# A sparse-attention decoder step on one core: the samples' index scores moved to the front, the prompt's index projections moved into the stage of the selection

## The reference, cut to what matters

```python
h = rmsnorm(x, W['mix_norm'][i])
aq, ak, av, iq, ik, iw, bq, bf, bi, bg = split(h @ w_in, IN_OFFSETS)
qi, ki = rope(iq, pos), rope(ik, pos)          # 8 heads x 64, and one shared key of 64
# scores: I[t,s] = sum_h w[t,h] * relu(qi[t,h] . ki[s])
# prompt: 1024 x 1024, causal.  sample: 4 queries x (8192 cached keys + 4 new ones)
_, idx = top_k(scores, 256)                    # then attention over the chosen keys alone
```

## Time and profile before

| | us |
|---|---|
| median of 3 runs | 3287.24 (3284.7 to 3288.15) |
| the profiled execution | 3285.84, its span 3284.0 |
| PE busy | 2955.7 (90%) |
| DVE busy | 1711.3 (52%) |
| ACT, POOL busy | 785.5 (24%), 492.2 (15%) |
| mean granted clock of PE | 0.952 |

### The profile page before, as it was taken

How to read it: one execution, slowest core, us unless ns; L and a number is a source line. 1 busy time by engine, 2 the same in 40 slices (tenths; PEclk the granted TensorE clock), 3 DMA queues, 4 the chain that set the end, 5 groups by cost and what they waited for, 6 DMA issues and landing times. The chain is left out here.

```text
span 3284.0 us, 41974 instructions
## 1 busy us (share of the span) xinstructions
PE 2955.7 (90%) x17344; PEld 2528.2 (77%) x17344; DVE 1711.3 (52%) x2105; ACT 785.5 (24%) x1121; POOL 492.2 (15%) x490
## 2 busy tenths in 40 slices
PE   6898999889688869999999999993699999999988
PEld 3593444464366749899999999892499999999988
DVE  2059998987476553433433343647633334344454
ACT  2132441142255511311111111320211111111232
POOL 1422335566442221000000000000000000000000
PEclk8899999899899979999999999996799999999999
DMA  2252120356511132111111111111011111111011
GB/s 90 59 155 79 53 80 8 112 166 184 184 34 37 35 105 68 56 52 40 47 45 52 39 52 34 33 33 52 31 40 51 52 40 52 40 52 40 28 51 68
DMA packets 160300, 207.62 MB, mean 63 GB/s; under 512 B 17127, under 2 KB 121231, under 8 KB 160094
## 3 DMA queue, kind: packets, MB, share of 16 engines
q1 hardware_dynamic: 145253, 154.38, 14.6%
q0 software_dynamic: 14848, 50.34, 5.2%
HBM read 182.13 MB, written 22.78 MB: 62 GB/s over the span
## 5 line engine op out<-in xcount | busy, mean ns | idle before, releaser
L1998 PE MATMUL ps<-h_split,w_split 128*128 128x352 f32 x7488 | 1215.5, 324 | 17.6 <-DVE w_split L2468 8.2
L1998 PEld LDWEIGHTS ps<-h_split,w_split 128*128 128x128 f32 x7488 | 1206.2, 189 | 24.5 <-issue 12.2
L1998 PE MATMUL ps<-hidden,w_split 128*128 128x352 f32 x3456 | 566.1, 323 | 0.0
L1998 PEld LDWEIGHTS ps<-hidden,w_split 128*128 128x128 f32 x3456 | 558.0, 188 | 0.0
L433 PE MATMUL ps<-w_chunk,hT 128*128 128x512 f32 (+3 forms) x1008 | 402.0, 553 | 26.7 <-DMA w_chunk<-in_w_in 26.7
L433 PEld LDWEIGHTS ps<-w_chunk,hT 128*128 128x128 f32 (+1 forms) x1008 | 169.9, 183 | 234.4 <-issue 202.8
L2506 DVE TENSOR_TENSOR xT<-xT,ps 128x1056 f32<-128x1056 f32 x176 | 220.5, 1253 | 203.0 <-PE ps L1998 202.8
L2485 DVE TENSOR_TENSOR hT<-hT,ps 128x1056 f32<-128x1056 f32 x44 | 55.0, 1254 | 361.2 <-PE ps L1998 361.2
L2359 ACT CAST w_split<-hT 128x2048 fp32r<-128x2048 f32 (+1 forms) x82 | 145.4, 1773 | 388.1 <-PE ps L1998 388.1
L2468 DVE TENSOR_TENSOR w_split<-hT,w_split 128x2048 fp32r<-128x2048 f32 (+1 forms) x82 | 175.0, 2134 | 80.4 <-ACT w_split L2359 79.2
L2495 DVE TENSOR_TENSOR hT<-hT,ps 128x1056 f32<-128x1056 f32 x44 | 55.2, 1255 | 233.4 <-PE ps L1998 233.4
(11 more groups left out here) (339 smaller groups left out, 3107.1 us busy)
## 6 DMA issues: line engine op xcount, KB each, us to landing
hT<-in_w_up SPq DMA_DIRECT2D x44, 1024.0 KB, 5.1
hT<-in_w_down SPq DMA_DIRECT2D x22, 1024.0 KB, 4.8
w_chunk<-in_w_in SPq DMA_DIRECT2D x6, 2048.0 KB, 8.4
hT<-in_w_ple_gate SPq DMA_DIRECT2D x16, 512.0 KB, 3.8
x_rows<-in_x_prompt SPq DMA_DIRECT2D x8, 512.0 KB, 4.5
w_gate_tile<-in_w_in SPq DMA_DIRECT2D x8, 512.0 KB, 5.3
w_out_raw<-in_w_out SPq DMA_DIRECT2D x8, 512.0 KB, 4.3
x_rows<-in_x_prompt SPq DMA_DIRECT2D x16, 256.0 KB, 2.6
```

The source lines that it names most:

```text
L1998: m = pe.matmul(out, w[a], x[b][:, g * GC:(g + 1) * GC], start=first and i == 0, stop=last and i == 2)
```

## The change

`load_normalised` and the stage of the projections of `iq` and `ik` are gone. `score_sample`, now in one stage with `lower_bound`, normalises the rows itself: the samples' tile first, the prompt's eight tiles between its other steps, the last six of them one in every two steps of the scoring loop. It loads the weights of `iq` and `ik`, projects the samples' 32 rows, rotates them on POOL, and scores. `select_sample` gets the prompt's jobs of `iq` and `ik` ahead of the others, eight each (61 jobs instead of 45), and the scores' steps begin at the third job of `av`. `EARLY_BIT` falls from 21 to 9.

```diff
-    jobs = [(c, r) for c in chunks for r in range(NT + 1)]
+    jobs = [(c, r) for c in chunks for r in range(NT if c in ("iq", "ik") else NT + 1)]
...
+        plain = starts[[c not in rotated for c in chunks].index(True)]
+        first = plain + LAG - 1
     def score_steps(j):
-        return range(2 * j, 2 * j + 2) if scores and 2 * j < len(index.steps) else range(0)
+        at = 2 * (j - first) if scores else 0
+        return range(at, at + 2) if scores and 0 <= at < len(index.steps) else range(0)
...
             for u in score_steps(j):
+                if u == 0:
+                    pe.wait_ge(copied, unplain)
                 index.tensor(pe, u)
...
-EARLY_BIT = 21
+EARLY_BIT = 9
...
 def score_sample(k, ctx, block):
     @block.sync
+        sp.dma_start(rows[0:NS, 0, :], io["x_sample"]...).then_inc(x_landed[0], 16)
+        sp.dma_start(w_iq, w_in[:, :, COL["iq"]:COL["iq"] + 512]).then_inc(w_landed[0], 16)
+        sp.dma_start(k.part[:], io["c_part"]).then_inc(pt_landed, 16)
         for s in range(8):
             sp.dma_start(pages[s:P:8, :]..., src).then_inc(pt_landed, 16)
+        sp.dma_start(w_ik[:], ...)
+        ...                                    # tables, x tiles 1 and 2
+        sp.wait_ge(iw_taken, 1)
+        ...                                    # the weights' round trip, the new index keys out
+        for t in range(3, NT + 1):
+            load_x(t)
     @block.gpsimd
+        for j in range(4):
+            gather(j)
+        rotate(0)
+        rotate(1)
+        for j in range(4, N):
+            gather(j)
     @block.tensor
+        turn_x(0)
+        project(0, w_iq, 512)
+        project(1, w_ik, IK_COLS)
+        turn(0)
+        turn_x(1)
+        turn(1)
+        turn_x(2)
+        ...                                    # turn the samples' key and queries, the new scores
+        for j in range(2, N + 2):
+            if j > 2 and j % 2 and LEAD + j // 2 - 1 <= NT:
+                turn_x(LEAD + j // 2 - 1)
             ...                                # turn(j), multiply(j - 2)
     @block.vector
         dve.wait_ge(pt_landed, 144)
         dve.tensor_scalar(index[:], pages[:], 8.0, k.part[:, 0:1], ...)
+        scale_x(0)
+        copy_x(0)
...
-    project_rows(k, ctx, block, chunks, scores=True, moves={3 * (NT + 1) + 1: move_lists})
+    project_rows(k, ctx, block, chunks, scores=True, moves={2 * NT + 3 * (NT + 1) + 1: move_lists})
...
-                    k.stage((load_normalised,), (lower_bound,))
-                    k.stage((project_rows, ["iq", "ik"]))
-                    k.stage((score_sample,))
-                    k.stage((select_sample, ["av", "bi", "bg", "aq", "ak"]))
+                    k.stage((lower_bound,), (score_sample,))
+                    k.stage((select_sample, ["iq", "ik", "av", "bi", "bg", "aq", "ak"]))
```

More of the change, by code:

```diff
@@ L172, in load_constants @@
     k.lb_logit = [k.vec[:, 8 * KD + i * BH:8 * KD + (i + 1) * BH] for i in range(2)]
[L177 to L243, removed]
@@ L334, in project_rows @@
     w_in = io["w_in"][0].rearrange("(k p) n -> p k n", p=P)
-    jobs = [(c, r) for c in chunks for r in range(NT + 1)]
+    jobs = [(c, r) for c in chunks for r in range(NT if c in ("iq", "ik") else NT + 1)]
+    starts = [jobs.index((c, 0)) for c in chunks] + [len(jobs)]
     rotated = {"aq", "ak", "iq", "ik"}
@@ L343, in project_rows @@
         index = k.index = PromptScores(k, ctx)
-        assert all(c not in rotated for c, _ in jobs[0:len(index.steps) // 2])
+        plain = starts[[c not in rotated for c in chunks].index(True)]
+        first = plain + LAG - 1
+        assert all(c not in rotated for c, _ in jobs[plain:first + len(index.steps) // 2])
     def score_steps(j):
-        return range(2 * j, 2 * j + 2) if scores and 2 * j < len(index.steps) else range(0)
+        at = 2 * (j - first) if scores else 0
+        return range(at, at + 2) if scores and 0 <= at < len(index.steps) else range(0)
     nth_rot, nth_store = {}, {}
@@ L371, in project_rows @@
     stored = k.sem_ring(ctx, "rows_stored", RAW)
-    projected, taken, roped, turned, copied, iw_stored = k.sems(
-        ctx, "projected", "taken", "roped", "turned", "copied", "iw_stored")
+    projected, taken, roped, turned, copied = k.sems(ctx, "projected", "taken", "roped", "turned", "copied")
+    chunk_of = [i for i in range(len(chunks)) for _ in range(starts[i], starts[i + 1])]
+    unplain = sum(starts[0] <= j < plain for j in nth_rot) if scores else 0
     def stores_before(j):
@@ L416, in turn @@
             pe.wait_ge(roped, t + 1)
-            if scores and t == 0:
+            if scores and t == unplain:
                 pe.wait_ge(index.rectified, len(index.steps))
@@ L483, in _ @@
     def _(pool):
-        if scores:
-            for u in range(len(index.steps)):
-                index.pool(pool, u)
         for j, (c, r) in enumerate(jobs):
+            if scores and j == plain:
+                for u in range(len(index.steps)):
+                    index.pool(pool, u)
             if c not in rotated:
@@ L1313, in score_sample @@
 def score_sample(k, ctx, block):
-    io, ps = k.io, k.ps
+    io, ps, hT = k.io, k.ps, k.hT
     N = BD * 4
     E16 = PAGE // 8
+    order = [NT] + list(range(NT))
+    LEAD = 3
+    w_iq = k.qT[:].rearrange("p f n -> p (f n)")[:, 0:KD * 512].rearrange("p (d n) -> p d n", d=KD)
+    room = k.kT[:].rearrange("p f n -> p (f n)")
+    rows = room[:, 0:3 * D].rearrange("p (s n) -> p s n", s=3)
+    square = room[:, 3 * D:4 * D]
+    stat = k.sb(ctx, "x_stat", [P, 3, 3])
+    w_ik = k.sb(ctx, "w_ik", [P, KD, IK_COLS])
+    raw = k.sb(ctx, "index_raw", [NS, 512 + DH])
+    rot = k.sb(ctx, "index_rot", [NS, 512 + 2 * DH])
+    rope_part = k.sb(ctx, "rope_part", [NS, 2, 512])
     pages = k.sb(ctx, "pages", [P, N], I32)
@@ L1359, in _, with gather @@
         view = io["cache_kidx"][0].rearrange("g (s e) d -> (g s) (e d)", s=8)
-        pool.wait_ge(indexed, 1)
-        for j in range(N):
+        def gather(j):
             if j >= 4:
@@ L1366, in _, with rotate @@
                                     ).then_inc(g_landed[j % 4], 16)
+        def rotate(n):
+            heads = 1 if n else H
+            cols, at = heads * DH, 512 * n
+            pool.wait_ge(taken, n + 1)
+            x = raw[:, at:at + cols].rearrange("p (h t d) -> p h t d", h=heads, t=2)
+            table = k.rope[0:NS, NT, :].rearrange("p (a t d) -> p a t d", a=2, t=2)
+            for a, v in ((0, x), (1, x[:, :, ::-1, :])):
+                pool.tensor_tensor(rope_part[:, a, 0:cols].rearrange("p (h t d) -> p h t d", h=heads, t=2), v,
+                                   table[:, a, :, :][:, None, :, :].broadcast_to([NS, heads, 2, DH // 2]), ALU.mult)
+            pool.drain()
+            if n:
+                pool.tensor_tensor(rot[:, at + cols:at + 2 * cols], rope_part[:, 0, 0:cols], rope_part[:, 1, 0:cols], ALU.add)
+            pool.tensor_tensor(rot[:, at:at + cols], rope_part[:, 0, 0:cols], rope_part[:, 1, 0:cols], ALU.add).then_inc(roped, 1)
+            pool.drain()
@@ L1368, in _ @@
+        pool.wait_ge(indexed, 1)
+        for j in range(4):
+            gather(j)
+        pool.wait_ge(sample_table, 16)
+        rotate(0)
+        rotate(1)
+        for j in range(4, N):
+            gather(j)
     @block.tensor
     def _(pe):
[L1370 to L1374, removed]
@@ L1375, in _, with turn_x @@
-        pe.matmul(ps[0:NS, 6, 0:NS * H].rearrange("p (b q) -> p b q", b=BD), k.ikT[0:DH, SEQ:R],
-                  bd[0:DH, :, 0].rearrange("p b t h -> p b (t h)"), start=True, stop=True).then_inc(new_scored, 1)
+        def turn_x(t):
+            r = order[t]
+            n = rows_of(r)
+            pe.wait_ge(x_scaled, t + 1)
+            if t:
+                pe.wait_ge(x_copied, t)
+            if t == LEAD:
+                pe.wait_ge(new_summed, 1)
+            for d in range(KD):
+                m = pe.transpose(ps[:, 6 + d // 4, (d % 4) * P:(d % 4) * P + n], rows[0:n, t % 3, d * P:(d + 1) * P], k.ident[0:n, 0:n])
+            m.then_inc(x_turned, 1)
@@ L1378, in turn, with project @@
+        def project(n, w, cols):
+            pe.wait_ge(w_landed[n], 16)
+            for d in range(KD):
+                m = pe.matmul(ps[0:NS, 2 + n, 0:cols], hT[:, d, SEQ:R], w[:, d, :], start=d == 0, stop=d == KD - 1)
+            m.then_inc(projected, 1)
         def turn(j):
@@ L1414, in _, with root, copy_keys @@
     def _(act):
-        for j in range(N):
+        def root(t):
+            n, s = rows_of(order[t]), t % 3
+            act.wait_ge(x_landed[s], 16 * (t // 3 + 1))
+            if t >= 3:
+                act.wait_ge(x_scaled, t - 2)
+            act.activation(square[0:n], rows[0:n, s, :], ACT.Square, accum_out=stat[0:n, s, 0:1])
+            act.drain()
+            act.activation(stat[0:n, s, 1:2], stat[0:n, s, 0:1], ACT.Sqrt, bias=k.eps[0:n, 0:1], scale=1.0 / D).then_inc(rooted, 1)
+        def copy_keys(j):
             for a in range(2):
```

123 lines of the change are left out of this document (98 added, 25 removed).

## The result

The changed kernel takes 3337.72 us (median of 4 runs, 3336.55 to 3340.04) where the kernel before took 3285.97 (4 runs beside it, 3283.25 to 3288.15): a ratio of 1.0159 [1.0141, 1.0176], slower. The forecast was 3327, its range 3308 to 3348. The profiled execution of after took 3336.55 us, with a span of 3334.8: 50.8 more than before.

A forecast was written before the change was run, and what follows sets the result against it. PE was taken to bound the scoring loop, PE and DVE together the selection, DVE ending it by some 4 us. Front -103.9, wait +73.2 and rounds +70.4 sum to +39.7 us: forecast 3327, range 3308 to 3348.

The forecast's parts named there:

- The front: Up to the selection's start: first weighing 110.1 us earlier, six tiles' transposes +6.2, so selection 103.9 us earlier, bounds 92 to 112.
- a sign that the prediction named for being wrong: Scoring loop: the forecast is wrong if its steps are longer than before by more than the transposes.
- rival 3: Front gains 22 us less, from a late page table and uncovered DVE and ACT tile work: 3349 us; chance 0.08.
- rival 4: Front gains more and the rounds are as short as they can be, 8 us: 3318, inside the forecast's range.
- The place of the lists: SP's queue in the selection: the lists stay behind the stores of `av`, `bi`, `bg`, which come 76.0 us later.
- the last turns of `ik`: PE in the selection: these turns and a wait for their copies add an estimated 1.1 us.
- The wait: DVE in the selection, ahead of the merge: a new wait of 73.2 us for the lists, bounds 68 to 78.
- The twelve rounds: End of the selection: twelve added threshold rounds without cover, 5.87 us each, 70.4 us; upper bound 81.6.
- The attention: Attention stage: loses twelve rounds, DVE idles about 96 us instead of 25.6, no gain counted, about 242 us as before.
- rival 2: Attention stage gives something back, at the very most PE's idle 32.7 us there: 3294; chance 0.04.
- Rival 1: Selection: the lists come in time, without the wait of 73 us; sum -15, 3272 us; chance 0.06.
- The spread: The forecast's own spread, 3312 to 3342 us, from the bounds of front, wait and rounds; chance 0.82.

The follow-up runs named there:

- the first experiment: Changed kernel with the DMAs of `cand` put ahead of job 34 and the spans' ahead of job 39, EARLY_BIT still 9: 3283.86 us, 0.9988 of the kernel before.
- the last experiment: Changed kernel with lists early, EARLY_BIT 21, seven table loads behind the first weights, and `ik` loaded ahead of `iq`: 3263.56 us, 0.9928 of the kernel before.
- The run before it: Changed kernel with lists early, EARLY_BIT 21, seven table loads behind the first weights, `iq` still ahead of `ik`: 3262.07 us, 0.992 of the kernel before.

## Why the prediction was right, step by step

**The front** was forecast to bring 103.9 us and brought 100.1. Its path was right to about a microsecond down to the first weighing (row numbers at 18.86 for 18.0, weighing at 47.08 for 46.0). The loop was not: from the first weighing to the last it takes 135.28 - 47.08 = 88.20 us, where it took 236.34 - 156.15 = 80.19 before, so 8.0 more instead of 6.2. 3.2 of them are the second step, 5.78 us behind the first (2.62 before), for which DVE waits 2.85 on PE. One of the six tiles lies in it, and PE works through it without a gap, but mostly at the lower of the clock's two levels; it had stood still three times for 1.3 to 1.8 us between 33.8 and 40.8. A tile's transposes in this step and in a later one, and the window of the step:

```profile
46.84 1.91 PE L1381 MATMUL ps<-ident,kT 128*128 128x128 f32 x8
...
55.49 1.09 PE L1381 MATMUL ps<-ident,kT 128*128 128x128 f32 x8
```

```profile
47.00:53.00 6.00, 6.00 (x37) 6.00 (x36) 2.74 (x4) 2.50 (x6) 0.93 (x1) 0.61 0.50 150
```

The kernel before was granted 1.00 in the same step (156 to 159 us). The other five tiles make a step 3.75 us instead of 2.62, 5.6 together, and one step at the end is 0.8 shorter. So the sum's 1.04 a tile was the price at the upper clock, and a sign that the prediction named for being wrong, a loop longer than before by more than the transposes, did come, by 1.8 us. DVE's and ACT's extra work was covered, as forecast (they are busy 72.19 and 50.62 of the 137 us from 6 to 143), so rival 3 falls; so does rival 4, the front being no better than the sum.

**The place of the lists**: 76.0 us of PE's added jobs were forecast, and `cand` was issued 80.6 later. The sum left out a queue: eight jobs of `ik` are short, so PE waits for their rotated keys,

```profile
228.71 1.90 PE L365 MATMUL ps<-w_chunk,hT 128*128 128x72 f32 x16
233.56 0.47 PE L354 MATMUL ps<-ident,rot 128*128 128x128 f32 x1 [2.95 <-POOL rot L442]
233.82 3.53 PE L365 MATMUL ps<-w_chunk,hT 128*128 128x72 f32 x16
```

and the tile behind that stop takes 3.53 us instead of 1.90, at a granted clock of 0.50 (233.6 to 237.4) instead of 1.00 (222 to 230). POOL itself was held up by ACT, which stood 6.2 us for a store of rotated keys:

```profile
231.79 0.18 ACT L392 ACTIVATE iw<-ps 128x8 f32<-128x8 f32 x1 [6.24 <-DMA out_kidx_prompt<-rot]
```

That store, issued at 223.90, stood behind the 2 MB of `av` in SP's queue (issued at 222.75). The small price for "the last turns of `ik`", 1.1 us, should have been some 6.

**The wait** was forecast at 73.2 us against where the lists stood before and measured at 77.5, in which DVE asked 5.5 us later, so that 72.0 are seen as idle time. (5.0 of the 5.5 lie in 16 pairs of short passes, L1645 and L1647, which take 8.4 and 11.7 us instead of 7.4 and 7.7; the prediction had DVE's passes unchanged.) The mechanism is the one named: with the lists issued early the wait is gone.

**The twelve rounds** were forecast at 70.4 us without cover, and the rounds cost 75.1 more. The size of the uncovered ones was right to the hundredth (597.06 to 602.93 is 5.87), and there were 13 of them; the ones beside POOL were sized too low, 6.8 where 9 rounds take (597.06 - 530.93) / 9 = 7.35. The average of before hid two kinds of rounds, and this is what is told of below. That the 5.87 was right is luck in part: the prediction read it in the earlier trace rows from the round that begins at 554.71, as one without rotations, but POOL rotated in that round too. POOL's timeline before, and DVE's at the end of the round:

```profile
555.29 2.50 POOL L502 TENSOR_TENSOR rope_part<-raw,rope 128x512 f32<-128x512 f32 x2 [3.56 <-ACT raw L459]
557.93 1.27 POOL L508 TENSOR_TENSOR rot<-rope_part 128x512 f32<-128x512 f32 x1
```

```profile
560.32 0.17 DVE L657 SCALAR_TENSOR_TENSOR threshold<-threshold,threshold_flip 128x6 int32<-128x6 int32 x1
```

The rotation ended at 559.20, before the round came to its two small updates (L655 at 560.08, then L657), and the round was as short as one without POOL.

**The attention** gave nothing back, so rival 2 falls: DVE's idle time ahead of the turned scores was 96.2 us with the rounds moved out and 23.7 with them in, as forecast, and the stage is 244 us either way. The gathers of keys after, in the list of a line's forms:

```profile
L1840 POOL DMA_INDIRECT gathered<-in_cache_k,slot_row x64: 940/953/2492, 676.4 to 790.0; - x64
```

Against 942, 952 and 2491 in the earlier trace rows: with none of the rounds beside them they are no quicker. The hold of GpSimd's gathers that the prediction took from the Trainium skill (SBUF — State Buffer, "SBUF: two separate sides") isn't seen here. The section itself gives the counting passes no such hold: it names VectorE's two-port modes for it, and leaves out of them the form of tensor_scalar that also writes out its accumulator, which these passes are.

**Rival 1**, the lists in time, wasn't this kernel but is the first experiment. It was priced at 3272, 15 below before, and came out 4.3 below. In that run the front is worth 4.2 less than in its sum (the selection starts at 143.93); the scores end 4.9 later against the selection's start (464.15 - 143.93 = 320.2 for 315.3, DVE waiting 7.0 for them); and the 22 rounds take 150.8 for 147. These three make 12.9 us where the time came out 10.7 above the rival's price.

The sum was +39.7 and the span says +50.8: 3.8 from the front, 4.3 from the lists and 4.7 from the rounds are 12.8 more; the way from the merge to the first round (57.4 us instead of 58.6) and the stage of the attention (244.5 instead of 245.0) take 1.7 back. The three errors point the same way, and the range, not the sum, took them in. The spread's upper end of 3342 was too low for its own bounds: 11.9 for the front, 4.8 for the wait and 11.6 for the rounds above 3327 make 3355.

## What to carry to other kernels

When work is added ahead of an entry in a queue that one engine goes through in order, ask who waits at the end of that entry: here 128 KB of lists (four DMAs of 32 KB) stood behind all the stores of `ik`, `av`, `bi` and `bg`, with which they had nothing to do. Moving them by ten jobs was worth 53.9 us with 22 rounds behind them, and 3.0 with ten. Work that is moved from a place where its engine idles to one where that engine ends the stage pays its full price there; here the place that it left gave nothing back. When two engines end a stage together, a repair of one chain is worth only what is left until the other ends it; size two repairs together before adding their gains.

## What the hardware showed that was not expected

**Rounds beside GpSimd take GpSimd's rhythm.** DVE's groups of the counting line and its two small updates, by form, from 531 to 597 (9 rounds beside rotations) and then from 597 to 673.6 (13 without), after (count | busy us, mean ns):

```profile
L571 DVE TENSOR_SCALAR_CACHE_REDUCE xT<-xT,threshold 128x1024 uint8<-128x1024 f32 x9 | 11.5, 1274 | 0.0
L591 DVE SCALAR_TENSOR_TENSOR threshold<-threshold,threshold_flip 128x6 int32<-128x6 int32 x9 | 10.3, 1145 | 0.7
...
L589 DVE TENSOR_SCALAR threshold_flip<-count 128x6 int32<-128x6 f32 x9 | 5.7, 630 | 1.0 <-issue 0.4
```

```profile
L571 DVE TENSOR_SCALAR_CACHE_REDUCE xT<-xT,threshold 128x1024 uint8<-128x1024 f32 x13 | 16.6, 1275 | 0.0
...
L589 DVE TENSOR_SCALAR threshold_flip<-count 128x6 int32<-128x6 f32 x13 | 2.2, 172 | 1.0
L591 DVE SCALAR_TENSOR_TENSOR threshold<-threshold,threshold_flip 128x6 int32<-128x6 int32 x13 | 2.2, 166 | 1.3 <-issue 0.4
```

The big passes, 1274 and 1275 ns, don't feel POOL at all, nor do they in the round of the earlier trace rows above, in which the whole rotation lay beside them. The two updates of six words a partition do: 630 + 1145 - 172 - 166 = 1437 ns a round, nearly the 7.35 - 5.87 = 1.48. And they end when POOL's two products end, here in DVE's timeline and POOL's:

```profile
595.82 1.14 DVE L591 SCALAR_TENSOR_TENSOR threshold<-threshold,threshold_flip 128x6 int32<-128x6 int32 x1
```

```profile
594.46 2.48 POOL L436 TENSOR_TENSOR rope_part<-raw,rope 32x512 f32<-32x512 f32 x2 [3.51 <-ACT raw L393]
```

595.82 + 1.14 = 596.96 and 594.46 + 2.48 = 596.94; in all nine rounds the two ends lie within 0.03 us. Once its updates meet the two products, a round of 5.87 us is tied to PE's job of 7.3, which paces POOL. The Trainium skill (the same section) says that VectorE and GpSimd share a port pair that one of them locks for a whole instruction, and that on VectorE's side a tensor_scalar in a two-port mode or an operation with two inputs in SBUF needs it, but not the tensor_scalar that also writes out its accumulator. The rows agree: the update of L591 has two inputs and L589's is a tensor_scalar (no row shows its mode), and they are held; the passes are the third kind and are not. That two updates of six words would set the pace of a round was not expected. It was read from traces and not tried apart.

**A busy PE at the lower clock.** In the last experiment PE worked from 160 to 180 us without a gap and was granted 0.57, running the tiles of `ik` up to 175.4; over all of them, from 147.1 to 175.0, it was busy 27.82 of 27.90 us at 0.50. The run before it, with tiles of `iq` from 160 to 180, was granted 1.00. An order chosen for an earlier start was paid for in clock. Why the clock stayed down was not tried.
